# A decoder block with routed experts: the rows of the experts' results are read back in another order and summed by other engines, and a small table is built earlier

## The reference, cut to what matters

```
scores = sigmoid(u2 @ w_router); biased = scores + router_bias
eidx   = the 8 best experts of a token, out of its 4 best groups of 8
gate   = scores[eidx] / sum * 2.5
routed[token] = sum over its 8 experts e of gate_e * ((silu(x @ w_gate[e]) * (x @ w_up[e])) @ w_down[e])
h   = h + gate2 * (routed + shared(u2))
out = rms_norm(h) * norm_f_g
```

## Time and profile before

| | us |
|---|---|
| median of three runs | 1203.81 |
| the profiled execution's own time | 1205.88 |
| its span, first to last instruction | 1204.1 |
| PE busy (92% of the span) | 1112.1 |
| DVE busy (44%) | 533.4 |
| POOL busy (20%) | 235.0 |
| ACT busy (15%) | 180.5 |

### The profile page before, as it was taken

One profiled execution on the slowest core, in us unless ns is written; L12 is line 12 of the kernel. 1 busy time (PEld: TensorE's weight loads), 2 busy tenths in 40 slices (PEclk: granted clock), 3 DMA queues, 4 the chain that ended last, 5 costly groups with the idle time before them and its releaser, 6 DMA issues.

```text
span 1204.1 us, 14748 instructions
## 1 busy us (share of the span) xinstructions
PE 1112.1 (92%) x5546; PEld 490.8 (41%) x5547; DVE 533.4 (44%) x1149; ACT 180.5 (15%) x385; POOL 235.0 (20%) x256
## 2 busy tenths in 40 slices
PE   4799899989999999998899999999999899998973
PEld 1344555433333444444333443444443344343331
DVE  0286766986933203436633333332323323332257
ACT  6212322231213000120000000000000000000001
POOL 6867393000000000020011211111111111111100
PEclk9899888999999999999999999999999999998987
DMA  9850441451341422025999999999999999999894
GB/s 344 223 192 19 158 135 22 158 208 37 140 155 35 160 87 70 36 79 217 371 407 420 417 416 416 414 419 418 419 420 404 411 422 376 408 397 404 327 412 172
DMA packets 87032, 323.45 MB, mean 269 GB/s; under 512 B 29400, under 2 KB 32472, under 8 KB 57264
## 3 DMA queue, kind: packets, MB, share of 16 engines
q1 hardware_dynamic: 67072, 282.93, 59.4%
q0 software_dynamic: 13488, 36.23, 7.7%
q10 hardware_dynamic: 6400, 3.33, 1.1%
HBM read 305.53 MB, written 28.33 MB: 277 GB/s over the span
## 4 chain that ended last, share of the span: by engine, by line
PE 61%; DMA 23%; DVE 11%; issue 2%; ACT 1%; SPq 1%; POOL 0%; ACTq 0%; DVEq 0%; POOLq 0%
PE ps L1668 18%; PE ps L2052 11%; DMA ring<-in_w_exp_up 5%; PE ps L2081 5%; DMA XT<-u_rows,idx 5%; PE ps L1927 5%; PE ps L1641 4%; PE ps L2019 4%; DMA ADA<-in_w_exp_down 3%; DMA ring<-in_w_exp_down 3%; PE ps L1788 3%; PE ps L2063 2%; DMA ADA<-in_w_exp_up 2%; PE ps L2169 2%; DMA ring<-in_w_ada 2%
## 5 line engine op out<-in xcount | busy, mean ns | idle before, releaser
L2052 PE MATMUL ps<-ring,XT 128*32 128x512 f32 (+1 forms) x1152 | 214.5, 596 | 9.4 <-DMA ADA<-in_w_exp_up 5.9
L1668 PE MATMUL ps<-uTs,ring 128*128 128x512 f32 (+1 forms) x416 | 185.3, 602 | 1.3 <-DVE sm L1290 1.3
L1496 DVE TENSOR_TENSOR uTs<-uTs,ps 128x256 f32<-128x256 f32 x44 | 18.5, 421 | 251.5 <-ACT uTs L1106 251.5
L1668 PEld LDWEIGHTS ps<-uTs,ring 128*128 128x128 f32 (+1 forms) x416 | 77.9, 191 | 100.5 <-issue 100.0
L2081 PE MATMUL ps<-ring,uTs 128*32 128x512 f32 (+1 forms) x576 | 110.8, 599 | 5.5 <-DVE uTs L1500 2.3
L843 POOL DMA_INDIRECT XT<-u_rows,idx x45 | 45.8, 1018 | 356.8 <-DVE idx L1485 328.6
L1544 DVE SCALAR_TENSOR_TENSOR uTs<-ps,gat,ADA 128x512 f32<-128x512 f32 x88 | 62.0, 746 | 117.0 <-PE ps L2081 82.4
L2052 PEld LDWEIGHTS ps<-ring,XT 128*32 128x32 f32 (+1 forms) x1152 | 62.4, 118 | 111.2 <-issue 108.3
L1106 ACT ACTIVATE uTs<-ps 128x256 f32<-128x256 f32 x44 | 16.9, 384 | 478.2 <-PE ps L2052 327.5
L2052 PE MATMUL ps<-ADA,XT 128*32 128x512 f32 (+1 forms) x320 | 87.1, 602 | 0.6 <-DMA ring<-in_w_exp_up 0.6
L2019 PE MATMUL ps<-ring,XT 128*128 128x512 f32 x192 | 84.4, 592 | 0.0
(11 more groups left out here) (354 smaller groups left out, 1381.1 us busy)
## 6 DMA issues: line engine op xcount, KB each, us to landing
ring<-in_w_exp_gate SPq DMA_DIRECT2D x52, 1024.0 KB, 15.1
ring<-in_w_exp_up SPq DMA_DIRECT2D x52, 1024.0 KB, 22.4
ring<-in_w_exp_down SPq DMA_DIRECT2D x52, 1024.0 KB, 23.5
ring<-in_w_ada SPq DMA_DIRECT2D x12, 2048.0 KB, 11.5
ring<-in_w_in SPq DMA_DIRECT2D x7, 2048.0 KB, 9.0
ADA<-in_w_exp_gate SPq DMA_DIRECT2D x12, 1024.0 KB, 16.5
ADA<-in_w_exp_up SPq DMA_DIRECT2D x12, 1024.0 KB, 22.8
ADA<-in_w_exp_down SPq DMA_DIRECT2D x12, 1024.0 KB, 24.1
```

The lines of the kernel that those rows point to most:

```text
L1668: ins = mm(b[0:rows_, 0:cols], l, r, start=(k == 0), stop=(k == len(chunks) - 1))
L2052: ins = mm(a3(ps[0][c, :], 2), xgT[par][:, k, c], wgu[r][:, k], start=(k == 0), stop=(k == KD - 1))
```

## The change

The eight iotas of `rank_of` move in POOL's program from behind the bias load to behind the attention's tables. `read_order` goes by tiles: quarters of tiles 0 and 1 as early as the scatters allow, then the rest tile by tile. PE sums quarters 0 and 1 and the first row of quarter 3 of each tile, and also the first row of quarter 2 of tile 3; DVE adds quarter 2 and the second row of quarter 3 (of tile 3 only the second row of quarter 2). DVE's and PE's orders follow.

```diff
-        read_order = [(t, q) for q in range(2) for t in range(TT)] + [(t, q) for t in range(TT) for q in range(2, 4)]
+        read_order = [(0, 0), (1, 0), (2, 0), (0, 1), (0, 2), (1, 1), (1, 2), (0, 3), (1, 3), (3, 0)]
+        read_order += [(2, 1), (2, 2), (2, 3), (3, 1), (3, 2), (3, 3)]
...
                 last.then_inc(S["dist"], 1)
+            lo = 0
+            while lo < NE:
+                hi = next((c for c in range(lo, NE) if RANK_OF[c] != RANK_OF[lo] + c - lo), NE)
+                E.iota(rank_of[:, lo:hi], [[1, hi - lo]], base=RANK_OF[lo], channel_multiplier=0, allow_small_or_imprecise_dtypes=True)
+                lo = hi
...
             E.iota(eid, [[0, P]], base=0, channel_multiplier=1, allow_small_or_imprecise_dtypes=True)
-            lo = 0
-            while lo < NE:
-                hi = next((c for c in range(lo, NE) if RANK_OF[c] != RANK_OF[lo] + c - lo), NE)
-                E.iota(rank_of[:, lo:hi], [[1, hi - lo]], base=RANK_OF[lo], channel_multiplier=0, allow_small_or_imprecise_dtypes=True)
-                lo = hi
...
-            for t in range(TT):
-                add_rows(t, 0, (0, 1))
-            for t in range(TT):
-                add_rows(t, 2, (0, 1) if t < TT - 1 else (0,))
-                if t:
-                    scaled(t - 1)
-                if t == TT - 1:
-                    add_rows(t, 2, (1,))
-                    add_rows(t, 3, (1,))
+            def sums_added(t):
+
                 for n in range(2):
                     c = slice(512 * n, 512 * (n + 1))
                     dve.wait_ge(S["sums_ok"], 2 * t + n + 1)
                     ins = V.tensor_tensor(H[:, t, c], H[:, t, c], ps[2 * t + n][:, :], ALU.add)
                 ins.then_inc(S["fin_add"], 1)
+
+            for t in range(2):
+                add_rows(t, 2, (0, 1))
+            for t in range(2):
+                add_rows(t, 3, (1,))
+                sums_added(t)
+            scaled(0)
+            add_rows(2, 2, (0, 1))
+            scaled(1)
+            add_rows(2, 3, (1,))
+            sums_added(2)
+            add_rows(TT - 1, 2, (1,))
+            scaled(2)
+            add_rows(TT - 1, 3, (1,))
+            sums_added(TT - 1)
             scaled(TT - 1)
...
-                                 start=(q == 1 and k == 0), stop=(q == 3 and k == ks[-1]))
+                                 start=(q == 0 and k == 0), stop=(q == 3 and k == ks[-1]))
...
-            for t in range(TT):
+            for t in range(2):
+                rows_summed(t, 0, (0, 1))
                 rows_summed(t, 1, (0, 1))
-            for t in range(TT):
-                rows_summed(t, 3, (0, 1) if t < TT - 1 else (0,))
+            for t in range(2):
+                rows_summed(t, 3, (0,))
+            for t in range(2, TT):
+                rows_summed(t, 0, (0, 1))
+                rows_summed(t, 1, (0, 1))
+                if t == TT - 1:
+                    rows_summed(t, 2, (0,))
+                rows_summed(t, 3, (0,))
```

## The result

| | before | changed |
|---|---|---|
| median of 5 runs, us | 1204.20 (1202.95 to 1205.23) | 1197.25 (1196.61 to 1200.15) |
| ratio | | 0.9948, 95% interval 0.9933 to 0.9963 |
| span of the profiled execution | 1204.1 | 1197.0 |

It is 7 us faster by the medians, 6.3 by the ratio, and 1196.8 was forecast. To see where the 7.1 us of the spans come from, I cut the traces at three points that every kernel here has: the start of the bias load (L816 before, L822 after), POOL's first scatter and its last.

What follows compares the result with a forecast made beforehand. It took POOL's chain before the expert stage, DMA and PE within it, and DVE's tail work as bounds. Table -0.8, reads 0 and split -6.2 sum to -7.0, 1196.8 us from 1203.8; range 1193.5 to 1200.7.

Steps and rivals of the forecast that it cites:

- The table: Ahead of the expert choice: eight iotas leave POOL's chain of waits, the expert stage starts earlier, -0.8 us.
- 1.6 us more go: Expert choice: if PE's shorter idle time leaves its clock at 2.4 GHz, 1.6 us extra gain, not counted in -0.8.
- the queue would not run dry: Tail reads: despite SP's moved waits, read 7's first bytes come at 1162.3, before the queue is empty.
- a gap in the DMA share between 1157 and 1165: Tail reads: a sign named in advance that would show the prediction wrong.
- The term that I had at 0: Tail reads: cost of the new order, put at 0 us, bounds -0.7 and +5.7; every position lands when it did.
- The end at 1190.8: Tail: PE's sums of 42 blocks, started at 1153.2, end at 1190.8 after 1.5 us of clock loss and 36.1 of work.
- the 1.5 us: Start of PE's tail sums: loss from 3.0 us at half clock, bounds 0 and 3.7 us.
- it never waits: PE's tail sums: rows always land in time, the tightest being (2,3), landing at 1178.1 and wanted at 1178.7.
- The floor that I gave: Tail: earliest end of PE's sums, set by read (2,3) and the work behind it, 1190.1.
- Better: Rival: PE starts by 1151 and is never slow, upstream clock stays up; 1193.8 to 1195.0 us; 14%.
- Eaten by the last scatter: Rival: read 7 takes 10.0 us from issue, PE ends at 1195.8, time 1201.8 us, no change that can be told; 5%.
- slower, at 1.2 GHz: Rival: PE runs the tail at half speed because its work comes in bursts between waits; about 1231 us; 4%.

Runs made afterwards that it cites:

- DVE with quarter 0: Changed kernel with quarter 0 of tiles 0 and 1 added by DVE, leaving PE 34 blocks instead of 42; 1197.49 us, 0.9942 of before.
- tail only: Kernel before with only the order of reads, order of sums and who adds what changed, table of ranks in its old place; 0.9953 of before.
- the balanced one: Changed kernel, DVE adding quarter 0 of tiles 0 and 1, PE summing in landing order, tile 2 scaled under ACT's squares of tile 3; 1196.16 us, 0.9930.

## Why the prediction was right, step by step

**The table.** -0.8 was right to 0.1 us at the first scatter. The bias load was no new wait. But what I had left out with the remark "1.6 us more go" if the clock stays up did happen, and was lost again at once: in all eight profiles with the early table and nothing filled the low clock of the choice is missing and one between 587 and 594 is there. Its price, 1.6 us (the first pass takes 8.67 us instead of 7.07), is the same. What I had not thought of is that a low clock can be moved rather than saved. Filling the two waits ahead of the new place took it away, so they have a part in it; but the same two waits were not followed by a low clock in the two kernels that have one in the choice. What links the two places stays open.

**The reads.** That the queue would not run dry was wrong, and with it one of the prediction's own signs of being wrong came true, a gap in the DMA share between 1157 and 1165: 0.17 from 1158 to 1160 and 0.53 in the two us after. The reasoning went by landings, one per 2.58 us. But (1,2) landed only at 1162.3, although the share, a mean over 16 engines, was 0.17 from 1158 on; so what was left of it stood, as I read it, with a few engines that were behind the others. The term that I had at 0 measures 0.8 us at (0,3), which landed at 1165.1 where 1165.2 less the 0.9 by which all was early is 1164.3. At (2,3), the read that came to bound, only 0.2 of it is left, and as much at the last read, since the reads behind (0,3) came 2.5 us apart instead of 2.58. The Trainium skill (DMA: Bandwidth & Descriptors, "Latency and other measured facts") says that two of the sixteen engines, 7 and 15, are usually slower than the others in traces; its guess at the cause is special to the path of DMAs that POOL issues, which these reads are not. Which engines were behind here no run shows.

**PE.** The end at 1190.8 (1189.9 with the earlier start) was met within 0.1 us, at 1189.8, by errors that cancel. PE began 1.3 us earlier than I took from DVE's row, and its clock stayed at 1.00, so that nothing of the 1.5 us was lost; then "it never waits" failed, with 1.6 us of waits, and the 42 blocks took 37.1 us instead of 36.1. (The low clock of the old tail, which the prediction puts at 7.3 us, lasted 6.8 in the trace.) The floor that I gave, read (2,3) and the 12 blocks of tile 3 behind it, was the bound: 1177.48 + 12.30 = 1189.8. DVE with quarter 0 shows it by taking 6.9 us from PE for nothing. The prediction had this floor 0.7 us under its own end and took the wrong one of the two for the bound.

**DVE.** It added its rows beside PE's sums as said, waiting for rows and sums, not holding them up, and the last sum ended at 1190.5 instead of 1197.7. The tail lost 6.18 us; -6.2 was forecast. That this agrees to 0.02 is luck, since against the two other profiles of the old tail it would be 7.2 and 7.7. From the last sum to the end 6.5 us passed, as before.

**The rivals.** "Better" came in one half: PE early and at full clock, while the upstream clock was handed back. "Eaten by the last scatter" and "slower, at 1.2 GHz" did not come: (0,3) took 5.0 us from its issue instead of 10.0, and the clock was 1.00 from PE's first sum to 1194. But the path of the first of these two, the last scatter's landing and the reads behind it, is the one that bounds the tail now. The Trainium skill (TensorE: Matmul & The Clock Gate, "HAM oscillation — how this bites in real kernels") describes groups of matmuls that start at the low clock after each wait for a load; the trace shows no such thing in PE's sums with their waits of 0.5 and 1.1 us. The low clock at 590 is another case: the waits ahead of it were for DVE, and in the kernel before the same waits were followed by the full clock.

## What to carry to other kernels

When partial results are read back and reduced, read them in the order that completes units of output, and look at what still stands behind the last but one read: the time was set by one read and the blocks queued behind it in program order, not by the sum of an engine's work. A low clock that goes from one place must be looked for at the next short waits before its gain is booked. Compare such parts between fixed points of two traces rather than by the totals, where 1 us can't be told here, and learn from several profiles how far a part spreads with the same code: 0.1 us up to the first scatter here, but 1.8 in the experts' stage and 1.5 in the old tail.

## What the hardware showed that I had not expected

- Low clock, at 0.50, by kernel: before and tail only at 548 to 553 and 981 to 987; the eight profiles with the table early and no filling at 587 to 594 and 932 to 942. All have one more near 1100. With the waits at 586 and 588 filled, the kernel with the changed tail has none between 540 and 1098, and the balanced one only that at 933 to 937. Waits of 2.98 and 2.99 us in the choice were followed by it, waits of 2.20 and 2.21 were not; PE's idle times of 4.5 to 5.3 us just before the tail's sums were, in five profiles, and those of 1.9 to 2.1 were not, in five. The waits of 1.11 and 1.52 us before the first pass were followed by it in nine profiles and not in two.
- A DMA share under 0.75 for 6 us, 0.17 at the lowest, put the next read off by 0.8 us and the one that bounds, five reads on, by 0.2.
- The last of the sixteen reads landed 2.6 to 4.0 us behind the one ahead of it in the profiles with the new order of reads, the others mostly 2.5; in the four with the old order it was 2.5 too. In the nine an output of 512 KB had been issued 7 to 13 us before that landing, in the four 2 to 3; whether that is the cause no run tests.
- The 44 scatters' landing was 8.2 to 10.0 us before, the last one's 8.7; it took 8.7 in the changed kernel as well, with the queue of reads nearly empty at its end.
